# Where a unit's second scores and its scaling stand in the instruction order of an encoder step

## The chip, the core and the metric

One core of a Trainium2 chip runs the whole program. The metric is device time in microseconds of one execution. Engines: PE (TensorE, matmuls and transposes), DVE (VectorE), ACT (ScalarE), POOL (GpSimd) and SP, which only issues DMAs. All data are float32. Wide products use three passes on split numbers (high times high, high times low, low times high), which is why nearly every operand exists as a "hi" and a "lo" tile.

## The reference

One inference step of a four-layer encoder for 1024 prompt tokens and 32 decoded tokens (1056 together) with 512 cached positions. Every layer does the same around a different token mixer:

```
h = rmsnorm(x);  u = h @ w_in                 # mixer columns, memory queries, gate
br = mixer(...)                               # layers 0 and 3: A, layer 1: B, layer 2: C
mo = softmax(mq mem_k^T) mem_v                # M: 4 heads, 256 memory tokens
x  = x + (concat(br, mo) * silu(gate)) @ w_out
```

- A: 12 heads of 64, chunk-causal over a band of nine chunks of 64, with a relative bias.
- B: 6 differential heads: softmax(q0 k0) - lam * softmax(q1 k1) times a value of width 128, then an RMS norm.
- C: 12 latent heads; queries and keys have 64 plain and 32 rotary columns.

## The kernel before

Python builds one list, `plan.order`, and each engine's program walks through that list and issues only its own instructions. So the list fixes the order on every engine at once, and semaphores join the engines. Nothing is scheduled at run time.

**Jobs and units.** Per layer, attention is eight jobs: two M jobs (two memory heads each), then six of the mixer (two heads each, or one differential head). A job has five units (`units_of`, L169): four groups g of 256 queries and one of the 32 decoded tokens (g = 4). The units run as 0, 1, 2, 3, 4 in M and as 0, 2, 1, 3, 4 in the mixers. Units are written here by kind and group, as A2 for group 2 of an A job. A group has two tiles of 128 queries, and `width` is the number of keys that a tile sees: in M 256 and 256; in A 128 and 256 (A0), 384 and 512 (A1), 640 and 640 (A2, A3); in B and C 128 and 256 (group 0), 384 and 512 (group 1), 640 and 768 (group 2), 896 and 1024 (group 3). The decoded unit has one tile, of 544 keys or, in M, of 256.

**Steps of a unit.** Items of the list, with the lines where each engine does its part:
- `S` (scores): PE multiplies queries with keys into two score banks per lane (L1383); DVE adds the bias and takes a row minimum of the negated scores (L1154); ACT takes the exponential with its sum (L956). A tile of up to 512 keys takes one bank, tile 0 bank 0 and tile 1 bank 1; a wider one takes both, and so must wait until the tile before it has been biased.
- `N` (the scaling): DVE only. It waits for the exponentials, takes reciprocals (L1166) and multiplies the probabilities (L1177 and L1178; in B L1170, L1172 and L1174).
- `turn` (one chunk): PE transposes up to four 128x128 blocks of probabilities into a PSUM bank (L1395); ACT copies them out as hi (L965), and DVE subtracts for lo (L1184). The first turn of a unit waits for the `N` of its last tile.
- `pv`: PE multiplies values with the turned chunk into acc bank 0 (L1425). `evac`: DVE multiplies the result into the gate (L1208; in B L1203).
- `vt` (the values' transposition): PE L1407, ACT L974, DVE L1192.
- `part`: side products. While a job runs, the operands of the next one (q, k, v; in C uqe, uqo, ck, cv) are computed on PE in acc bank 1 (L1362), each a sum of 3 times 8 matmuls in A and B, which can be cut into 2 or 3 parts over the chunks. ACT reads each out (L875).
- `wsplit`: ACT makes w_hi (L915), POOL w_lo (L1228). `conv`: DVE casts the next job's queries and keys (L1136), POOL subtracts (L1246). `rot`: three DVE instructions that rotate C's queries (L1021, L1022, L1024). `vconv`: the cached values' split. `bsum` and `bmul`: B's norm (PE L1435, ACT L986 and L989, DVE L1215).

**The pipeline.** `unit` (L356) interleaves. While the chunks of unit u are turned and multiplied, the next unit nxt is scored and scaled. At chunk 0 stand the last `pv` of the unit before, its `evac`, the scores of nxt's tile 0, the values' transposition, the first part, and only then the scores of nxt's tile 1. Later chunks do `turn`, `pv` of the chunk before, and parts. The number n of chunks is 2 in M and 1 in the decoded units; A0 has 2, A2 and A3 have 5, A1 has 4; B0 has 1, B1 2, B2 3, B3 4; C0 has 2, C1 4, C2 6, C3 8. In units with n = 1 the `N` items stand behind all parts; with n = 2 they stand at the very end, behind the last part, the second `vt` and, in group 3, the first `conv`; with more chunks they stand in front of `turn`'s `pv` (tile 0, chunk 1) and behind it (tile 1, chunk 2).

Of the kernel before, what the change touches and what calls it, by code (L numbers as in the profile page):

```python
# [194 lines left out]
class Plan:  # L195
# [160 lines left out]
    def unit(self, u, prev, nxt, sides, jobs):  # L356

        order = self.order
        job, n = u.job, len(u.chunks)
        at = job.units.index(u)  # L360
        following = next((j for j in jobs if j.n == job.n + 1), None)
        parts = [[] for _ in range(n)]
        for i, s in enumerate(sides):
            own = list(range(n))[n * i // len(sides):n * (i + 1) // len(sides)] or [n * i // len(sides)]
            for p, c in enumerate(own):
                parts[c].append((s, p, len(own)))
        two = nxt is not None and len(nxt.tiles) == 2
        turns = [] if job is jobs[0] else list(range(len(V_TURNS[job.kind])))
        after_b = prev is not None and prev.job.kind == "B"
        if at == 4 and following is not None:  # L370
            order.append(("bprep", following))
        for c in range(n):
            self.turn(u, c)
            if c == 0:
                if prev is not None:
                    self.times_v(prev, len(prev.chunks) - 1)
                    order.append(("evac", prev))
                if nxt is not None:
                    self.scores(nxt, 0)
                if at == 0 and turns:  # L380
                    self.v_turn(job, 0)
                if at == 0 and following is not None:
                    order.append(("kload", following))
                if at == 3 and following is not None:
                    order.append(("bload", following))
                if parts[0]:
                    self.part(*parts[0][0])
                if two:
                    self.scores(nxt, 1)
                for x in parts[0][1:]:  # L390
                    self.part(*x)
                if n == 1 and nxt is not None:
                    order += [("N", nxt, t) for t in range(len(nxt.tiles))]
                if at == 1 and job is not jobs[0] and job.kind in "AB":
                    order.append(("vconv", job))
            else:
                if c == 1 and n > 2 and nxt is not None:
                    order.append(("N", nxt, 0))
                self.times_v(u, c - 1)
                if c == 2 and two:  # L400
                    order.append(("N", nxt, 1))
                if at == 3 and following is not None and c in (1, 3 if n > 4 else 2):
                    order.append(("conv", following, 0 if c == 1 else 1))
                for x in parts[c]:
                    self.part(*x)
            if after_b and c == min(1, n - 1):
                self.sum_of_squares(prev)
            if after_b and c == min(3, n - 1) and n != 2:
                order.append(("bmul", prev))
            if at == 0 and len(turns) > 1 and c == min(1, n - 1):  # L410
                self.v_turn(job, 1)
            if at == 1 and c < len(turns) - 2:
                self.v_turn(job, c + 2)
            if at == 1 and c == n - 1 and following is not None:
                order.append(("vload", following))
        if n == 2 and nxt is not None:
            order += [("N", nxt, t) for t in range(len(nxt.tiles))]
        if n == 2 and after_b:
            order.append(("bmul", prev))
        if at == 3 and following is not None and n == 2:  # L420
            order.append(("conv", following, 1))

# [1140 lines left out]
```

## Time and profile before

| what | us |
|---|---|
| median of 3 runs | 3563.18 |
| lowest and highest | 3560.32, 3565.85 |
| the profiled execution | 3553.51 |
| its span | 3551.7 |
| PE busy in it | 2924.7 (82%) |
| DVE busy | 1576.1 (44%) |
| ACT busy | 1221.1 (34%) |
| POOL busy | 832.2 (23%) |

The mean granted clock of TensorE in that execution was 0.884 of full speed. Busy time is what an engine spent in its instructions. In the views that list instructions, a bracket at the end of a row says how long the engine had been idle before it and which instruction let it go on.

### The profile page before, as it was taken

The numbers are of one execution on the slowest core, as the hardware profiler recorded it, in microseconds if no ns is written. First come the engines' busy times: TensorE is split into PE (matmuls) and PEld (weight loads), VectorE is DVE, ScalarE is ACT, GpSimd is POOL, SyncE is SP. The second block draws the span as 40 slices with busy tenths as digits, with TensorE's granted clock in tenths as the row PEclk, the third lists the DMA queues.
The fourth block names the chain that finished last, engine by engine and source line by source line (L and its number), as shares of the span: only waits on it lengthen the run. The fifth ranks groups of instructions, "written<-read, shape, count | busy, mean of one in ns | idle before, by whom it ended". The sixth has DMA issues, their size and how long they took to land.

```text
span 3551.7 us, 46359 instructions
## 1 busy us (share of the span) xinstructions
PE 2924.7 (82%) x18786; PEld 2708.6 (76%) x18786; DVE 1576.1 (44%) x3502; ACT 1221.1 (34%) x2680; POOL 832.2 (23%) x434
## 2 busy tenths in 40 slices
PE   5888899979888888869887667777779979999877
PEld 4787888869887777759787566666668978888777
DVE  7114555552215666661223256566551035555552
ACT  3323333332223444442232233333332233333331
POOL 7412112112412121213311222222104312122102
PEclk8998989989998999979997788788789989999979
DMA  3211111103111111103110000000013111111111
GB/s 140 91 42 47 38 38 47 38 26 122 56 36 52 43 51 43 55 20 120 60 36 31 24 10 8 6 8 6 13 64 94 44 33 47 41 52 38 47 61 61
DMA packets 55892, 167.90 MB, mean 47 GB/s; under 512 B 6464, under 2 KB 14272, under 8 KB 55168
## 3 DMA queue, kind: packets, MB, share of 16 engines
q1 hardware_dynamic: 55680, 164.94, 13.8%
q8 instruction: 149, 2.44, 0.3%
q14 instruction: 63, 0.52, 0.0%
HBM read 131.13 MB, written 33.79 MB: 46 GB/s over the span
## 4 chain that ended last, share of the span: by engine, by line
PE 68%; DVE 17%; ACT 8%; POOL 3%; issue 3%; DMA 0%; SPq 0%; DVEq 0%; ACTq 0%
PE acc L1362 32%; PE scores L1383 9%; PE acc L1425 9%; PE acc L1341 8%; PE turned L1395 5%; ACT prob L956 3%; DVE prob L1154 3%; DVE prob L1177 2%; PE scores L1294 2%; POOL h_split L1236 2%; DVE pt_split L1184 2%; DVE raw L1042 2%; DVE prob L1178 1%; ACT pt_split L965 1%; DVE prob L1172 1%
## 5 line engine op out<-in xcount | busy, mean ns | idle before, releaser
L1362 PE MATMUL acc<-h_split,w_hi 128*128 128x352 f32 (+3 forms) x5116 | 1280.8, 334 | 70.2 <-POOL w_lo L1228 40.1
L1362 PEld LDWEIGHTS acc<-h_split,w_hi 128*128 128x128 f32 x5116 | 915.0, 198 | 91.4 <-POOL w_lo L1228 43.5
L1228 POOL TENSOR_TENSOR w_lo<-w_raw,w_hi 128x1024 fp32r<-128x1024 f32 (+2 forms) x172 | 389.9, 2270 | 2013.0 <-ACT w_hi L915 2012.9
L1362 PE MATMUL acc<-h_split,w_lo 128*128 128x352 f32 (+3 forms) x2558 | 840.9, 329 | 0.0
L956 ACT ACTIVATE prob<-prob,stat 128x256 f32<-128x256 f32 (+9 forms) x576 | 386.7, 672 | 608.4 <-DVE stat L1154 608.4
L1425 PE MATMUL acc<-pt_split,v_split 128*64 128x256 f32 (+4 forms) x3486 | 515.4, 290 | 70.7 <-DVE pt_split L1184 64.7
L1395 PE MATMUL turned<-ident,prob 128*128 128x128 f32 (+2 forms) x1866 | 311.0, 294 | 298.6 <-DVE prob L1178 218.1
L1184 DVE TENSOR_TENSOR pt_split<-turned,pt_split 128x512 fp32r<-128x512 f32 (+4 forms) x564 | 303.0, 552 | 488.1 <-ACT pt_split L965 487.0
L1154 DVE CUSTOM_DVE_ANT_0 prob<-scores,bias 128x256 f32<-128x256 f32 (+9 forms) x576 | 343.3, 634 | 388.8 <-PE scores L1383 385.2
L1362 PEld LDWEIGHTS acc<-h_split,w_lo 128*128 128x128 f32 x2558 | 503.9, 197 | 0.0
L1395 PEld LDWEIGHTS turned<-ident,prob 128*128 128x128 f32 (+2 forms) x1866 | 229.0, 152 | 351.6 <-DVE prob L1178 235.7
L1425 PEld LDWEIGHTS acc<-pt_split,v_split 128*64 128x64 f32 (+1 forms) x3486 | 417.2, 168 | 95.4 <-DVE pt_split L1184 84.7
L965 ACT ACTIVATE pt_split<-turned 128x512 fp32r<-128x512 f32 (+4 forms) x564 | 260.9, 481 | 469.7 <-PE turned L1395 468.1
L1383 PE MATMUL scores<-k_split,q_split 64*128 64x512 f32 (+10 forms) x2196 | 355.0, 392 | 62.1 <-DVE stat L1154 31.6
L1383 PEld LDWEIGHTS scores<-k_split,q_split 64*128 64x128 f32 (+3 forms) x2196 | 232.3, 216 | 134.3 <-issue 61.1
L1341 PE MATMUL acc<-h_split,w_hi 128*128 128x352 f32 x1152 | 280.2, 327 | 9.2 <-POOL w_lo L1228 9.2
L915 ACT ACTIVATE w_hi<-w_raw 128x1024 fp32r<-128x1024 f32 (+2 forms) x172 | 166.5, 972 | 297.9 <-PE acc L1341 219.9
L1341 PEld LDWEIGHTS acc<-h_split,w_hi 128*128 128x128 f32 x1152 | 203.4, 192 | 10.2 <-issue 10.2
L1136 DVE CAST q_split<-q_raw 128x256 fp32r<-128x256 f32 (+1 forms) x52 | 28.1, 540 | 386.2 <-ACT q_raw L875 386.2
L1341 PE MATMUL acc<-h_split,w_lo 128*128 128x352 f32 x576 | 187.3, 325 | 0.0
L1294 PE MATMUL scores<-h_split,w_hi 128*128 128x352 f32 x512 | 133.8, 346 | 52.4 <-POOL h_split L1236 39.8
L1099 DVE TENSOR_TENSOR y_sb<-acc,y_sb 128x352 f32<-128x352 f32 x72 | 37.8, 525 | 253.5 <-PE acc L1341 253.5
(102 smaller groups left out, 2844.6 us busy)
## 6 DMA issues: line engine op xcount, KB each, us to landing
w_raw<-w SPq DMA_DIRECT2D x148, 512.0 KB, 3.5
x_scr<-y_sb SPq DMA_DIRECT2D x24, 528.0 KB, 5.3
y_sb<-x_scr SPq DMA_DIRECT2D x24, 528.0 KB, 5.4
bias<-rel_in SPq DMA_DIRECT2D x24, 320.0 KB, 4.2
raw<-kcache SPq DMA_DIRECT2D x18, 256.0 KB, 3.7
v_cache<-vcache SPq DMA_DIRECT2D x18, 256.0 KB, 3.7
y_sb<-x_in SPq DMA_DIRECT2D x8, 528.0 KB, 5.8
y_out<-raw SPq DMA_DIRECT2D x8, 528.0 KB, 2.7
```

Of the source, the lines that this page charges most:

```text
L915: act.activation(w_hi[:, n % 2, 0:wide], w_raw[:, n % 2, 0:wide], ACT.Copy).then_inc(whi_made.mark(n), 1)
L956: act.activation(p, p, ACT.Exp, scale=-1.0, bias=stat[0:tile.rows, i:i + 1], accum_out=stat[0:tile.rows, 8 + i:9 + i]).then_inc(exps_ready ...
L965: ins = act.activation(pt[0:rows, chunk.p % 2, 0, c0:c0 + n], t_ps[chunk.a % 2][0:rows, c0:c0 + n], ACT.Copy)
L1154: dve.tensor_tensor_reduce(out=prob[0:tile.rows, at:at + tile.width], in0=s_ps[lane][0:tile.rows, tile.at:tile.at + tile.width], in1=bias[ ...
L1184: ins = dve.tensor_tensor(pt[0:rows, chunk.p % 2, 1, c0:c0 + n], t_ps[chunk.a % 2][0:rows, c0:c0 + n], pt[0:rows, chunk.p % 2, 0, c0:c0 + ...
L1228: pool.tensor_tensor(w_lo[:, n % 2, 0:wide], w_raw[:, n % 2, 0:wide], w_hi[:, n % 2, 0:wide].bitcast(F32), ALU.subtract).then_inc(wlo_made ...
L1294: ins = pe.matmul(pair_banks[3 * i + c][:, 0:n], (w_hi, w_lo)[ws][:, w % 2, 128 * k:128 * k + 128], x[:, xs, k, a:a + n], start=k == 0 and ...
L1341: ins = pe.matmul(acc[i % 2][:, 0:n], (w_hi, w_lo)[ws][:, w % 2, 128 * k:128 * k + 128], h_v[:, xs, k, a:a + n], start=k == 0 and y == 0, ...
L1362: ins = pe.matmul(acc[s.bank][:, 0:s.cols], (w_hi, w_lo)[ws][:, w, 128 * k:128 * k + 128], x(xs, k), start=k == 0 and y == 0, stop=k == s. ...
L1383: ins = pe.matmul(s_ps[lane][0:tile.rows, tile.at + col:tile.at + col + n], q[rows, qs, tile.q0:tile.q0 + tile.rows], k[rows, ks, key:key ...
L1395: ins = pe.transpose(t_ps[chunk.a % 2][0:n, to:to + rows], prob[0:rows, at:at + n], ident[0:rows, 0:rows])
L1425: ins = pe.matmul(acc[0][0:width, dst:dst + w], v_sp[0:n, vs, block, 64 * lane:64 * lane + width], pt[0:n, chunk.p % 2, ps, src:src + w], ...
```

## The change

Only `unit` is changed. The scores of a next unit whose tiles are all at most 512 keys wide are issued for both tiles together, ahead of the values' transposition and of the first part. Where the next unit has one tile or is narrow, a unit with n = 1 issues `N` ahead of the parts; otherwise `N` follows the second scores directly. In units with n = 2 both `N` items move from the end to directly behind the second `turn`. With more chunks, the second `N` moves from behind `pv` to ahead of it. `bmul` of a unit with n = 2 moves into the loop. The order of the units, the table of side products per unit and all five engine programs are the same as before.

```diff
+        narrow = two and max(t.width for t in nxt.tiles) <= 512
         for c in range(n):
             self.turn(u, c)
             if c == 0:
...
                 if nxt is not None:
                     self.scores(nxt, 0)
+                if narrow:
+                    self.scores(nxt, 1)
...
+                if n == 1 and nxt is not None and not (two and not narrow):
+                    order += [("N", nxt, t) for t in range(len(nxt.tiles))]
                 if parts[0]:
                     self.part(*parts[0][0])
-                if two:
+                if two and not narrow:
                     self.scores(nxt, 1)
+                if n == 1 and two and not narrow:
+                    order += [("N", nxt, t) for t in range(2)]
                 for x in parts[0][1:]:
                     self.part(*x)
-                if n == 1 and nxt is not None:
-                    order += [("N", nxt, t) for t in range(len(nxt.tiles))]
...
             else:
-                if c == 1 and n > 2 and nxt is not None:
+                if c == 1 and nxt is not None:
                     order.append(("N", nxt, 0))
+                if c == (1 if n == 2 else 2) and two:
+                    order.append(("N", nxt, 1))
                 self.times_v(u, c - 1)
-                if c == 2 and two:
-                    order.append(("N", nxt, 1))
...
-            if after_b and c == min(3, n - 1) and n != 2:
+            if after_b and c == min(3, n - 1):
                 order.append(("bmul", prev))
...
-        if n == 2 and nxt is not None:
-            order += [("N", nxt, t) for t in range(len(nxt.tiles))]
-        if n == 2 and after_b:
-            order.append(("bmul", prev))
         if at == 3 and following is not None and n == 2:
             order.append(("conv", following, 1))
```

## Rows read from the trace of the kernel before

**Rows 1.** The page's busy times, then its chain that ended last, by engine.

```profile
PE 2924.7 (82%) x18786; PEld 2708.6 (76%) x18786; DVE 1576.1 (44%) x3502; ACT 1221.1 (34%) x2680; POOL 832.2 (23%) x434
...
PE 68%; DVE 17%; ACT 8%; POOL 3%; issue 3%; DMA 0%; SPq 0%; DVEq 0%; ACTq 0%
```

**Rows 2.** Waits of PE: us in total, times, longest us; last row 339:800 alone.

```profile
PE turned L1395 <- DVE prob L1178: 218.1, 64, 7.5
PE turned L1395 <- DVE prob L1174: 74.6, 24, 6.5
PE acc L1425 <- DVE pt_split L1184: 64.7, 45, 4.3
...
PE turned L1395 <- DVE prob L1178: 48.3, 12, 4.4
```

**Rows 3.** Timeline, one boundary into A0: start, us, instruction [idle before it].

```profile
491.14 0.55 PE L1383 MATMUL scores<-k_split,q_split 64*128 64x128 f32 x6
...
495.64 0.62 PE L1383 MATMUL scores<-k_split,q_split 64*128 64x256 f32 x6
...
497.20 2.46 DVE L1177 TENSOR_SCALAR prob<-prob,stat 128x128 f32<-128x128 f32 x1
497.23 2.34 POOL L1228 TENSOR_TENSOR w_lo<-w_raw,w_hi 128x1024 fp32r<-128x1024 f32 x1 [4.61 <-ACT w_hi L915]
...
500.63 1.12 PE L1395 MATMUL turned<-ident,prob 128*128 128x128 f32 x4 [4.37 <-DVE prob L1178]
501.40 3.58 PE L1425 MATMUL acc<-pt_split,v_split 128*64 128x32 f32 x30
...
504.91 2.18 PE L1383 MATMUL scores<-k_split,q_split 64*128 64x512 f32 x12
```

**Rows 4.** Timeline, the next boundary of such a job, from A0 into A2.

```profile
437.33 0.49 DVE L1184 TENSOR_TENSOR pt_split<-turned,pt_split 128x128 fp32r<-128x128 f32 x2 [1.39 <-ACT pt_split L965]
...
439.05 0.60 PE L1407 MATMUL turned<-ident,raw 128*128 128x128 f32 x4
...
440.32 0.69 DVE L1192 TENSOR_TENSOR v_split<-turned,v_split 128x512 fp32r<-128x512 f32 x1 [2.50 <-ACT v_split L974]
...
442.71 0.55 DVE L1178 TENSOR_SCALAR prob<-prob,stat 128x640 f32<-128x640 f32 x1
443.31 1.03 PE L1395 MATMUL turned<-ident,prob 128*128 128x128 f32 x4 [3.66 <-DVE prob L1178]
```

**Rows 5.** Timeline, B: the boundary into B0, then the one into B3.

```profile
1213.73 2.33 DVE L1172 TENSOR_SCALAR prob<-prob,stat 128x128 f32<-128x128 f32 x1
...
1217.61 0.69 PE L1395 MATMUL turned<-ident,prob 128*128 128x128 f32 x2 [4.32 <-DVE prob L1174]
...
1269.76 0.47 PE L1395 MATMUL turned<-ident,prob 128*128 128x128 f32 x1 [5.58 <-DVE prob L1174]
```

**Rows 6.** Timeline, C: the boundary into C0, then the one into C2.

```profile
2164.32 1.12 PE L1395 MATMUL turned<-ident,prob 128*128 128x128 f32 x4 [2.93 <-DVE prob L1178]
...
2184.54 1.25 DVE L1021 TENSOR_TENSOR raw<-q_even_raw,rope_sb 32x1056 f32<-32x1056 f32 x1 [1.44 <-ACT q_even_raw L875]
...
2187.52 1.25 DVE L1024 TENSOR_TENSOR q_even_raw<-q_even_raw,raw 32x1056 f32<-32x1056 f32 x1
...
2191.93 1.12 PE L1395 MATMUL turned<-ident,prob 128*128 128x128 f32 x4 [7.49 <-DVE prob L1178]
```

**Rows 7.** Timeline, M: around the decoded unit (M3 to M4), and into M2.

```profile
278.13 1.60 POOL L1246 TENSOR_TENSOR k_split<-raw,k_split 128x512 fp32r<-128x512 f32 x1
...
278.50 1.66 DVE L1136 CAST q_split<-q_raw 128x800 fp32r<-128x800 f32 x1
278.63 0.43 PE L1395 MATMUL turned<-ident,prob 32*128 32x32 f32 x4 [3.33 <-DVE prob L1178]
...
1058.01 0.66 PE L1395 MATMUL turned<-ident,prob 128*128 128x128 f32 x4 [1.11 <-DVE prob L1178]
```

**Rows 8.** Stretches: length, busy (x) of PE, PEld, DVE, ACT, POOL; PEclk, DMA, GB/s.

```profile
419.60:498.10 78.50, 71.04 (x517) 66.04 (x517) 40.18 (x104) 30.19 (x71) 14.43 (x9) 0.91 0.12 43
498.10:508.30 10.20, 7.67 (x52) 7.18 (x53) 4.56 (x11) 0.82 (x3) 1.48 (x1) 0.50 0.23 79
443.40:446.90 3.50, 3.50 (x18) 2.95 (x19) 1.84 (x4) 0.60 (x1) 0.00 (x0) 0.51 0.00 0
1214.90:1225.10 10.20, 7.49 (x36) 7.00 (x37) 4.96 (x13) 1.50 (x5) 1.08 (x1) 0.50 0.24 78
```

## The prediction

> **What bounds the kernel now.** The page first: PE is busy 82% of the span and carries 68% of the chain that ended last, DVE 17% [rows 1]. So PE sets the time, and what counts is where it stands still. The list of waits says on whom: 292.7 us (218.1 + 74.6) before a unit's first turn, on DVE's scaling, and 64.7 us before `pv`, on DVE's lo split [rows 2]. The timeline then places the first sum. I read it job by job, and every job of a kind repeats to 0.1 us, except the last of each layer, which has no side products. In the six A jobs of layer 0 there are 12 such waits of together 48.3 us (the last of [rows 2]), and layer 3 gives the same row: 4.37 us into each A0 [rows 3] and 3.66 into each A2 [rows 4]. B waits 4.32 into B0 and 5.58 into B3 [rows 5]; C 2.93 into C0 and 7.49 into C2 [rows 6]; M's first job of a layer 1.11 into each of three units [rows 7]. Elsewhere in an A job PE runs without a break: 71.04 us busy in a period of 78.5 [rows 8].
>
> The stretches show a second cost. Behind the wait at A0 the granted clock is 0.50 (the 1.2 GHz level) for 10.2 us, of which PE is busy 7.67; behind the one at A2 3.5 us at 0.51; behind the one at B0 10.2 us with 7.49 busy [rows 8]. The rest of the A job is at the upper level.
>
> **The change part by part.** No instruction is added or removed; each engine issues the same ones in another order. All counts are of this kernel's jobs.
>
> *Into A0 (12 times) and B0 (6).* Before: scores of tile 0 at 491.14, the v part between, scores of tile 1 at 495.64, so the part lasts 495.64 - 491.69 = 3.95 us. Then everything up to the first turn is exposed. It is long because the w_lo split on POOL (2.34 us) starts with DVE's scaling, and the 128-wide L1177 takes 2.46 us [rows 3], against 0.55 for a 640-wide L1178 [rows 4]. After: both scores stand together, the scaling is DVE's next work, and the part runs over it. The chain without the split is the old one, 500.63 - 496.26 = 4.37, less about 2.1 (2.46 less some 0.35, an estimate from the 0.55 of the wide one), so 2.3, and 0.6 more because tile 1 queues behind tile 0 on DVE and ACT: 2.9 us under a part of 3.95. No wait is left, and 1 us of slack. Gain 12 x 4.37 + 6 x 4.32 = 52.4 + 25.9 = 78. The split of w now falls behind the scaling, beside the lo split L1184.
> The GPSIMD Engine Reference of the Trainium skill (Key points) says that POOL's memory interface contends with Vector instructions in a two-port mode or with two SBUF inputs; L1177 beside L1228 agrees, and by that rule L1184, which reads PSUM, is not held.
>
> *A0 into A2 (10, and 2 without parts).* DVE ends the lo split of the second turn at 437.82, then idles until the values' transposition, issued by PE behind the part at 439.05, has come back as L1192 at 440.32; only then it scales, to 443.26 [rows 4]. After: scaling directly from 437.8. It takes 443.26 - 440.93 = 2.3 us (it overlaps L1192's end), so it ends at 440.15, and PE is ready at 439.65. The wait falls from 3.66 to 0.5: 10 x 3.1 = 31, and 0.7 each in the two jobs without a part, whose chain has only L1192 to lose: 1.4. L1192 moves behind the scaling, but its PSUM tile is only there at 440.3, so nothing waits for it: 32.
>
> *C0 into C2 (5 with the rotation; the layer's last job has none).* Before the scaling stand `rot` from 2184.54 to 2188.77 and L1192; the wait is 7.49 [rows 6]. The scaling fills the rest, 2191.93 - 2188.77 - 0.7 = 2.5 us. After: it starts when `rot` could, at 2184.5 less 1.44 idle = 2183.1 [rows 6], and ends at 2185.6; PE is ready at 2191.93 - 7.49 = 2184.44, so the wait falls to about 1. But `rot` (4.2), L1192 (0.7) and then the lo split of C2's first turn queue behind it on DVE, to 2191.2, and C2's second pair of transposes waits for that. PE has some 5 us of work until then (`pv`, two scores, a part), which before began only after the wait and now lies beside DVE's. So most of the 6.5 us are kept. The bounds are 1 (all of it late again at that turn) and 6.5; I take 5.5, nearer to the upper end, because the lo split that PE waits for would come at 2191.2, while before it could not start until ACT had read a transpose issued at 2191.93. 5 x 5.5, and 0.7 for the last job: 28.
>
> *C4 into C0 (5).* The cover is a cv part of 6 matmuls, 1.3 us, so 2.93 falls by 1 to 1.3: 5.
>
> *M (first job of each layer, three units).* The scores of tile 1 come 2.1 us earlier (half an mq part), but the turn in between pins the scaling behind its own lo split: of 1.11 [rows 7] 0.85 goes: 12 x 0.85 = 10. M3 to M4: the scaling passes the first `conv`. It gains 0.7 of 3.33, but the casts and POOL's two k and q splits start 0.9 later, the 800-wide cast that already stood 1.66 us beside POOL moves with them [rows 7], and the next job's first scores wait for POOL. Net loss 0.7 x 4 = 3, between 0 and 1.5 each.
>
> *No change:* into B3 (5.58) and B2: in both, between the old and the new place of `N` DVE has nothing, so its queue is the same. Tile 1's `N` ahead of `pv` is also nothing, since `pv` has no DVE part. `bmul` stays behind the same scaling. DMAs: SP's queue keeps its order, and w_raw's load follows the w_lo split as before.
>
> Stalls: 78 + 32 + 28 + 5 + 10 - 3 = 150. From this I take 5 for what shows up late next in C and around vconv, between 0 and 30: 145.
>
> **Rivals.**
> - *Stalls go, the clock stays.* For it: the 32-column matmuls. Against: in all 12 jobs the lower level begins inside the wait. 3563 - 145 = 3418. Chance 0.20.
> - *The whole lower level goes.* 3563 - 145 - 89 = 3329. Chance 0.14. "TensorE: Matmul & The Clock Gate" of the Trainium skill ("What's actually happening") says that the throttled state is the default and activity releases it, which would favour this one; that the lower level begins in the waits [rows 8] agrees.
> - *The moved scaling does nothing*, since ACT's exponentials and not L1192 or `rot` hold it. Against: L1192's idle bracket of 2.50 [rows 4]. Then 78 + 5 + 10 and half of the clock's 68 at A0 and B0: 3563 - 93 - 34 = 3436. Chance 0.07.
> - *What queues behind the scaling comes due elsewhere* (rot, L1192, conv): C and A2 give nothing, M loses, and the clock returns by half: 78 + 5 + 27 = 110 less 10, 3463. Chance 0.07.
> - *Slower: the scaling meets POOL.* Each meeting on the path costs 2.46 - 0.35 = 2.1 us [rows 3]. Today it meets 18 times. The order gains 200, so it turns slower from about 100 new meetings, of 172 splits of weights; at 110 it is 3563 - 200 + 231 = 3594. Against: most splits are issued behind a part's end, and the scaling now comes before. Chance 0.02.
> - *No effect beyond measurement:* chance 0.02.
>
> **How the numbers follow.** The forecast has 0.48 (its own range 3343 to 3393). Within 0.2% (7 us) is what a measurement of this kernel can't tell from no change. With the clock's two extremes, 3329 and 3418, 0.82 is covered; the range 3310 to 3432 holds them with their spread. Faster: all but 0.04; same 0.02, slower 0.02.
>
> **What would show it.** The waits of L1395 on L1178 and L1174 fall from 292.7 to about 110 (5.6 x 6 for B3, the M0 units at about 3, rests of 0.5 at A2, 1 to 1.9 in C). Right for A0: no bracket before its first turn, L1177 at 0.3 us, L1228 later than the scaling. Right for the clock: the stretch behind A0 at 0.9 or more, the mean over 0.91 against 0.884. Wrong: L1395 waiting at C2's second chunk for L1184 by 5 us or more, first scores of an M job waiting for POOL's k_split by over 2, or a clock that is still 0.50 behind A0.

## The result and the profile after

| | before | after |
|---|---|---|
| median, us (runs) | 3561.75 (4) | 3319.51 (4) |
| lowest, highest | 3554.15, 3565.85 | 3315.72, 3320.09 |
| the profiled execution | 3553.51 | 3319.59 |
| its span | 3551.7 | 3317.7 |
| PE busy in it | 2924.7 | 2822.7 |

The ratio is 0.932, with a 95% interval of 0.9302 to 0.9337. The lines of the kernel after stand one further down than before (L1395 is L1396, L1178 is L1179). From the page of the kernel after, its busy times:

```profile
PE 2822.7 (85%) x18786; PEld 2631.0 (79%) x18786; DVE 1540.5 (46%) x3502; ACT 1216.2 (37%) x2680; POOL 834.4 (25%) x434
```

Beside [rows 1] the counts are the same, so this is the same work. The span is 234.0 shorter: PE is busy 102.0 less, which must be the clock, as the instructions are the same, and idle 132.0 less (3551.7 - 2924.7 = 627.0 before, 495.0 after). The waits of PE in the kernel after (us in total, times, longest):

```profile
PE turned L1396 <- DVE prob L1179: 86.2, 55, 3.7
...
PE turned L1396 <- DVE prob L1175: 54.9, 24, 7.1
...
PE scores L1384 <- issue: 30.8, 8, 6.5
...
PE acc L1363 <- ACT w_rest L876: 13.4, 5, 2.7
```

The two waits on the scaling, 292.7 in [rows 2], are 141.1: 151.6 less. Two lines stand against that: `w_rest` is new (13.4), and "issue" was 24.6. These 13.4 + 6.2 = 19.6 are what is missing to 132.0: no other line of the list changes by more than 3.2, and together they change by 0.8.

One boundary into A0, to be read beside [rows 3] (start, us, instruction, idle before):

```profile
460.63 0.95 PE L1384 MATMUL scores<-k_split,q_split 64*128 64x128 f32 x12
...
463.17 0.29 DVE L1178 TENSOR_SCALAR prob<-prob,stat 128x128 f32<-128x128 f32 x1
...
464.42 0.35 DVE L1179 TENSOR_SCALAR prob<-prob,stat 128x256 f32<-128x256 f32 x1
...
465.48 0.60 PE L1396 MATMUL turned<-ident,prob 128*128 128x128 f32 x4
...
465.84 2.05 PE L1426 MATMUL acc<-pt_split,v_split 128*64 128x32 f32 x30
...
467.17 2.37 POOL L1229 TENSOR_TENSOR w_lo<-w_raw,w_hi 128x1024 fp32r<-128x1024 f32 x1 [5.07 <-ACT w_hi L916]
467.61 0.69 DVE L1185 TENSOR_TENSOR pt_split<-turned,pt_split 128x512 fp32r<-128x512 f32 x1 [2.84 <-ACT pt_split L966]
467.82 1.25 PE L1384 MATMUL scores<-k_split,q_split 64*128 64x512 f32 x12
```

Both tiles' scores stand in one row of 12. The scaling is over at 464.77, 0.7 before PE gets to the turn, which has no bracket. POOL's split starts 2.4 behind the scaling. The 30 short matmuls take 2.05 instead of 3.58.

Stretches of the kernel after (length, PE busy and its count, PEclk, DMA, GB/s): the 10.2 us behind that turn, then five periods of A in layer 0, of B, of C, and of A in layer 3, each from the first job's first turn of group 0 to the last job's:

```profile
465.48:475.68 10.20, 10.20 (x97) 1.00 0.30 106
...
334.97:662.79 327.82, 324.36 (x2567) 1.00 0.15 52
1053.00:1408.74 355.74, 315.52 (x2170) 0.95 0.15 53
1941.40:2397.26 455.86, 353.90 (x2157) 0.86 0.03 9
2809.64:3137.53 327.89, 324.43 (x2567) 1.00 0.15 52
```

The same periods in the kernel before:

```profile
343.05:739.80 396.75, 355.26 (x2567) 0.91 0.13 43
1140.58:1531.68 391.10, 332.82 (x2171) 0.91 0.14 48
2069.58:2556.57 486.99, 360.38 (x2158) 0.83 0.03 8
2973.30:3368.09 394.79, 353.29 (x2568) 0.92 0.13 43
```

Length less busy is idle, so each row parts its gain in two:

| five periods | shorter | idle less | busy less |
|---|---|---|---|
| A, layer 0 | 68.9 | 38.0 | 30.9 |
| B | 35.4 | 18.1 | 17.3 |
| C | 31.1 | 24.7 | 6.5 |
| A, layer 3 | 66.9 | 38.0 | 28.9 |

In A the clock is 1.00 over the whole stretch: nothing of the lower level is left. In C it only goes from 0.83 to 0.86.

### The profile page after: what moved, and what is told of

Its sections match the earlier page's. It is cut to its first block, busy times and chain, and to the rows that moved or that the text cites. A ratio compares the mean times of both kernels' runs of the same rounds, so it can differ in the third digit from the quotient of the medians.

```text
span 3317.7 us, 46359 instructions
## 1 busy us (share of the span) xinstructions
PE 2822.7 (85%) x18786; PEld 2631.0 (79%) x18786; DVE 1540.5 (46%) x3502; ACT 1216.2 (37%) x2680; POOL 834.4 (25%) x434
## 4 chain that ended last, share of the span: by engine, by line
PE 64%; DVE 17%; ACT 10%; issue 4%; POOL 4%; DMA 1%; SPq 0%; DVEq 0%; ACTq 0%
PE acc L1363 30%; PE acc L1342 9%; PE acc L1426 8%; PE scores L1384 8%; PE turned L1396 5%; ACT prob L957 5%; DVE prob L1155 3%; DVE pt_split L1185 3%; PE scores L1295 2%; POOL h_split L1237 2%; DVE raw L1043 2%; ACT pt_split L966 2%; DVE prob L1178 2%; DVE prob L1175 1%; POOL w_lo L1229 1%
## 5 line engine op out<-in xcount | busy, mean ns | idle before, releaser
L1363 PE MATMUL acc<-h_split,w_hi 128*128 128x352 f32 (+3 forms) x5116 | 1263.3, 330 | 84.4 <-POOL w_lo L1229 40.6
L1363 PEld LDWEIGHTS acc<-h_split,w_hi 128*128 128x128 f32 x5116 | 899.6, 194 | 109.0 <-POOL w_lo L1229 44.4
L1426 PE MATMUL acc<-pt_split,v_split 128*64 128x256 f32 (+4 forms) x3486 | 487.4, 280 | 73.5 <-DVE pt_split L1185 63.5
L1363 PEld LDWEIGHTS acc<-h_split,w_lo 128*128 128x128 f32 x2558 | 496.2, 194 | 0.0
L1426 PEld LDWEIGHTS acc<-pt_split,v_split 128*64 128x64 f32 (+1 forms) x3486 | 389.2, 156 | 98.5 <-DVE pt_split L1185 81.0
L1396 PE MATMUL turned<-ident,prob 128*128 128x128 f32 (+2 forms) x1866 | 301.4, 287 | 147.4 <-DVE prob L1179 86.2
L1396 PEld LDWEIGHTS turned<-ident,prob 128*128 128x128 f32 (+2 forms) x1866 | 227.2, 149 | 197.4 <-DVE prob L1179 103.8
L1384 PE MATMUL scores<-k_split,q_split 64*128 64x512 f32 (+10 forms) x2196 | 316.9, 364 | 69.3 <-DVE stat L1155 32.5
L1384 PEld LDWEIGHTS scores<-k_split,q_split 64*128 64x128 f32 (+3 forms) x2196 | 212.4, 200 | 125.0 <-issue 55.5
L1342 PEld LDWEIGHTS acc<-h_split,w_hi 128*128 128x128 f32 x1152 | 203.2, 192 | 10.2 <-issue 10.2
```

Of the source, the lines that this page charges most:

```text
L1342: ins = pe.matmul(acc[i % 2][:, 0:n], (w_hi, w_lo)[ws][:, w % 2, 128 * k:128 * k + 128], h_v[:, xs, k, a:a + n], start=k == 0 and y == 0, ...
L1363: ins = pe.matmul(acc[s.bank][:, 0:s.cols], (w_hi, w_lo)[ws][:, w, 128 * k:128 * k + 128], x(xs, k), start=k == 0 and y == 0, stop=k == s. ...
L1384: ins = pe.matmul(s_ps[lane][0:tile.rows, tile.at + col:tile.at + col + n], q[rows, qs, tile.q0:tile.q0 + tile.rows], k[rows, ks, key:key ...
L1396: ins = pe.transpose(t_ps[chunk.a % 2][0:n, to:to + rows], prob[0:rows, at:at + n], ident[0:rows, 0:rows])
L1426: ins = pe.matmul(acc[0][0:width, dst:dst + w], v_sp[0:n, vs, block, 64 * lane:64 * lane + width], pt[0:n, chunk.p % 2, ps, src:src + w], ...
```

## The experiments

The first three start from the kernel before: the first two do one part of the change each, the third moves only the split of w. The others start from the kernel after. Each time stands beside runs of the kernel before on the same chip (medians 3556.75, 3556.18 and 3556.41 in the three groups), and its ratio is to those.

**One part alone: the narrow scores together.**

```diff
+        narrow = two and max(t.width for t in nxt.tiles) <= 512
...
                     self.scores(nxt, 0)
+                if narrow:
+                    self.scores(nxt, 1)
...
-                if two:
+                if two and not narrow:
                     self.scores(nxt, 1)
```

> The kernel before with one part of the change alone: a narrow next unit's two score tiles are issued together; every scaling keeps its old place. Theory W (each wait brings its own stretch at the lower clock level, and takes it along when it goes): the waits into A0 and B0 go (about 76 us), M and C0 give 15, and the two lower stretches behind A0 and B0 return 68, so about 3403, with the 3.66 us wait into A2 and its 3.4 us at the lower level still there. Rival J (the level only comes back when all waits of a job are gone, or the 30 matmuls of 32 columns hold it down by themselves): about 3471, and the clock behind A0 still 0.50.

Measured: 3387.41, ratio 0.9527 (0.9511 to 0.9544), 169 us less. The stretches behind the turn into A0 and behind the one into A2:

```profile
478.54:488.74 10.20, 10.20 (x96) 1.00 0.31 106
496.76:500.26 3.50, 3.50 (x20) 0.50 0.00 0
```

Its terms had added up to 159 (76, 15 and 68), so it gave 10 more; PE is busy 82.6 less (2842.1), where 68 stood for the clock. The wait into A0 is gone and its lower stretch with it; A2's wait of [rows 4] is still 3.66 and keeps its own, which here lasts from 495.88 to 502.71. So each lower stretch belongs to its wait. The 30 short matmuls stand in the first of these rows at 1.00: their size does not hold the clock down.

**The other part alone: the scaling moved.**

```diff
-                for x in parts[0][1:]:
-                    self.part(*x)
                 if n == 1 and nxt is not None:
                     order += [("N", nxt, t) for t in range(len(nxt.tiles))]
+                for x in parts[0][1:]:
+                    self.part(*x)
...
-                if c == 1 and n > 2 and nxt is not None:
+                if c == 1 and nxt is not None:
                     order.append(("N", nxt, 0))
-                self.times_v(u, c - 1)
-                if c == 2 and two:
+                if c == (1 if n == 2 else 2) and two:
                     order.append(("N", nxt, 1))
+                self.times_v(u, c - 1)
...
-            if after_b and c == min(3, n - 1) and n != 2:
+            if after_b and c == min(3, n - 1):
...
-        if n == 2 and nxt is not None:
-            order += [("N", nxt, t) for t in range(len(nxt.tiles))]
-        if n == 2 and after_b:
-            order.append(("bmul", prev))
```

> The kernel before with the other part alone: the scaling moved as in the change, the second scores at their old place. Theory W: the wait into A2 falls from 3.66 to 0.4 (39 us) and its lower stretch goes (21), C2 gives about 32, the M4 units cost 3, so about 3473; A0 keeps its 4.37 us and its 10 us at 0.50. Rival J: no clock returns, about 3494. The savings of this one and of the scores alone should add to about 242, the whole change.

Measured: 3484.49, ratio 0.9798 (0.9781 to 0.9816), 72 less, where its terms (39, 21 and 32, less 3) had added up to 89. The clock gave what was expected: PE is busy 21.5 less (2903.2). The idle time did not: it is 47.1 less, where 68 stood. A2's wait is 0.46 and C2's 1.08, and the waits before first turns fall by 63.5 in all (to 154.4 + 74.8), but 16.4 of these come back elsewhere, 6.4 of them before the uqo part (`w_rest`) and 6.4 before the next M job's scores. Into A0 it shows what [rows 3] showed:

```profile
488.87 2.47 DVE L1173 TENSOR_SCALAR prob<-prob,stat 128x128 f32<-128x128 f32 x1
488.90 2.35 POOL L1224 TENSOR_TENSOR w_lo<-w_raw,w_hi 128x1024 fp32r<-128x1024 f32 x1 [4.61 <-ACT w_hi L911]
...
492.31 1.12 PE L1391 MATMUL turned<-ident,prob 128*128 128x128 f32 x4 [4.37 <-DVE prob L1174]
```

Beside their own runs of the kernel before the parts take 4.73% and 2.02%, together 6.75%, and the whole change takes 6.8%: the parts add up.

**Only the split of w behind the scaling.** In the decoded units and in B0 (n = 1), the scores stay apart.

```diff
+                    later = [x for x in order[mark:] if x[0] in ("wsplit", "wload")]
+                    order[mark:] = [x for x in order[mark:] if x[0] not in ("wsplit", "wload")] + later
```

> The kernel before with the weight split and the next weight load moved behind the scaling in the units of one chunk (A4, B4, C4), nothing else. It takes DVE's scaling away from POOL's split and ACT's w_hi from in front of the exponentials. If the 2.1 us beside POOL is a real price: waits into A0 and B0 fall from 4.4 to about 2.1, 41 us. If a wait of 2.1 us still brings the lower level: about 3521. If it doesn't: about 3453. If the overlap with POOL costs nothing on the path (the exponentials end last): 3555 or more.

Measured: 3519.76, ratio 0.9906 (0.9883 to 0.9928), 37 less, as the reading said by which a wait of 2.1 still brings the lower level (3521). The boundary into A0, and the stretch behind it:

```profile
493.56 0.29 DVE L1180 TENSOR_SCALAR prob<-prob,stat 128x128 f32<-128x128 f32 x1
...
495.14 1.12 PE L1398 MATMUL turned<-ident,prob 128*128 128x128 f32 x4 [2.51 <-DVE prob L1181]
...
495.90 3.58 PE L1428 MATMUL acc<-pt_split,v_split 128*64 128x32 f32 x30
```
```profile
495.03:501.80 6.77, 6.66 (x48) 0.50 0.33 116
```

The scaling beside POOL cost 4.37 - 2.51 = 1.86, and the prediction took 2.1. The edit also takes ACT's w_hi (1.05) from in front of tile 1's exponentials, but that is not what the wait was: in the kernel before these end at 498.13, and DVE, held beside POOL, is free for them only at 499.77. The clock is still at 1.2 GHz behind the shorter wait, and the short matmuls still take 3.58; that their size is not the reason, the first run shows and not this one.

**Is C2's new wait the scores' doing?** The kernel after has 2.7 for `w_rest` in C2. Its scores of C1 apart again:

```diff
-        narrow = two and max(t.width for t in nxt.tiles) <= 512
+        narrow = two and max(t.width for t in nxt.tiles) <= 512 and not (job.kind == "C" and at == 1)
```

> The kernel after, but in C2 units the two score tiles of C1 stand apart again, as before. Theory A (the new 2.7 us wait of the uqo part is ACT's queue: the exponentials of both score tiles stand ahead of the read that frees the bank, and wait for DVE's rotation): 5 x 2.7 = 13 less, 3306. Rival D (DVE's queue behind the rotation holds PE in any order): within 3 us of the kernel after, 3319.

Measured: 3322.08, ratio 0.9341 (0.9324 to 0.9357), no difference from the kernel after. It is not the place of C1's scores. The wait only splits up:

```profile
2054.92 0.51 PE L1363 MATMUL acc<-h_split,w_hi 128*128 128x264 f32 x2 [1.28 <-ACT w_rest L876]
...
2056.80 0.66 PE L1408 MATMUL turned<-ident,raw 128*128 128x128 f32 x4 [1.12 <-DVE v_split L1193]
```

**Is it the rotation, then?** Head 0's rotation (three operations of DVE) taken out of DVE's queue there and put behind the turn of C2's chunk 3; `streaming` is true inside `unit` only:

```diff
+            if s.what == "uqe" and self.streaming:
+                self.rot_later = ("rot", s.job, 0)
+            elif s.what in ("uqe", "uqo"):
...
             self.turn(u, c)
+            if c == 3 and self.rot_later:
+                order.append(self.rot_later)
+                self.rot_later = None
```

> The changed kernel, with one thing moved: the rotation of head 0 of the next C job, which DVE computes during C0's second chunk's turn and after (some 4.2 us of DVE, in four operations), is put behind the turn of C2's chunk 3, a unit in which DVE has room. Theory (DVE's queue holds PE at C0 to C2): in the changed kernel TensorE waits there 1.6 us at C2's second turn and 2.7 us for the uqo part, both behind that rotation; with it gone 2 to 4 us go in each of 5 jobs, so 10 to 20 us, 3300 to 3310. Rival (the rotation only moves the wait: the lo splits of C2 and the parts' evacuations queue behind it in its new place): within 3 us of the changed kernel, 3317 to 3323, with waits for L1185 in C2 longer than 1 us.

Measured: 3307.09 (3304.75 to 3307.59), ratio 0.9296 (0.9281 to 0.9311), 12.4 less than the kernel after. First the kernel after, then this one, from the rotation's last operation (in this one, from the lo split) to the uqo part:

```profile
2051.06 1.25 DVE L1025 TENSOR_TENSOR q_even_raw<-q_even_raw,raw 32x1056 f32<-32x1056 f32 x1
...
2055.02 0.61 ACT L957 ACTIVATE prob<-prob,stat 128x384 f32<-128x384 f32 x1 [5.19 <-DVE stat L1155]
...
2057.64 0.37 ACT L876 ACTIVATE w_rest<-acc 128x264 f32<-128x264 f32 x1
...
2058.06 0.39 PE L1363 MATMUL acc<-h_split,w_hi 128*128 128x264 f32 x1 [2.69 <-ACT w_rest L876]
```
```profile
2048.85 0.69 DVE L1193 TENSOR_TENSOR pt_split<-turned,pt_split 128x512 fp32r<-128x512 f32 x1 [0.78 <-ACT pt_split L974]
...
2053.55 0.37 ACT L884 ACTIVATE w_rest<-acc 128x264 f32<-128x264 f32 x1
...
2053.97 0.51 PE L1371 MATMUL acc<-h_split,w_hi 128*128 128x264 f32 x2 [0.60 <-ACT w_rest L884]
```

DVE's lo split now stands right behind its turn. The readout comes 4.1 earlier, 1.0 of it because C2's turn itself does (2047.52 against 2048.54). So the chain is: rotation, then DVE's bias for C1's tiles, then ACT's exponentials (idle 5.19 for them), and only behind these ACT's readout of the part, which frees the acc bank. The rotation starts it.

**The third M unit in the old order.**

```diff
+                held = n == 2 and at == 3
-                if c == 1 and nxt is not None:
+                if c == 1 and nxt is not None and not held:
...
+        if n == 2 and at == 3:
+            order.append(("N", nxt, 0))
```

> The changed kernel, with the scaling and transposition of the values of M4 put back behind the first convolution in the third M unit alone (M1, M2 keep the new order). Theory (the change loses a little there: M4's unit gets 0.8 us less wait at its own turn but the next job's first scores then wait 1.6 us for GpSimd's k_split): the wait at S(M0,0) goes from 1.58 to 0 and M4's goes from 2.50 back to 3.33; that is 0.75 us x 4 to 8 units, 3 to 6 us less than the changed kernel: 3314 to 3317. Rival (the two waits are one, whichever place it stands at): no difference, 3319 +- 2.

Measured: 3318.62 (3316.66 to 3322.26), ratio 0.9333 (0.9317 to 0.9348): no difference. First the kernel after, then this one:

```profile
273.18 0.43 PE L1396 MATMUL turned<-ident,prob 32*128 32x32 f32 x4 [2.50 <-DVE prob L1179]
...
274.70 1.26 POOL L1247 TENSOR_TENSOR k_split<-raw,k_split 128x512 fp32r<-128x512 f32 x1
...
276.06 1.65 PE L1384 MATMUL scores<-k_split,q_split 64*128 64x256 f32 x12 [1.58 <-issue]
```
```profile
273.44 1.60 POOL L1250 TENSOR_TENSOR k_split<-raw,k_split 128x512 fp32r<-128x512 f32 x1
...
273.94 0.63 PE L1399 MATMUL turned<-ident,prob 32*128 32x32 f32 x4 [3.32 <-DVE prob L1182]
...
275.98 1.65 PE L1387 MATMUL scores<-k_split,q_split 64*128 64x256 f32 x12
```

The next job's scores start at 276.06 or 275.98. What M4's turn gains, 0.82, its scores wait for again, since POOL's k_split ends 0.9 later (275.96 against 275.04). The wait of 1.58 put down to "issue" ends 0.1 behind that k_split.

**B3's wait, by POOL.** 5.58 into B3 is untouched by the change. The split in the two-chunk B unit moved behind the next unit's first turn:

```diff
             self.turn(u, c)
+            order += self.split_later
+            self.split_later = []
...
+                if job.kind == "B" and n == 2:
+                    self.split_later = [x for x in order[mark:] if x[0] in ("wsplit", "wload")]
+                    order[mark:] = [x for x in order[mark:] if x[0] not in ("wsplit", "wload")]
```

> The changed kernel, with GpSimd's split of the k part (its subtraction and the load behind it) moved in the wide B unit of two chunks from that unit's end to behind the first turn of the next one. Theory (the 5.58 us into B3 are DVE's 1024-wide scaling held beside GpSimd's subtraction, 2.50 us for 0.8): the wait falls by about 1.65 us to some 4.0, x5 jobs 8 us, 3311; if the lower clock behind that wait shortens too, up to 3305. Rival (the wait is set by the exponentials and sums, not by GpSimd): wait stays 5.5, time 3318 to 3322.

Measured: 3320.97, ratio 0.9336 (0.9321 to 0.9351). Here the mechanism held and the time did not move. The scaling before it in the kernel after, then in this one with the turn:

```profile
1238.49 2.50 DVE L1173 TENSOR_SCALAR prob<-prob,stat 128x1024 f32<-128x1024 f32 x1
...
1242.38 1.11 PE L1396 MATMUL turned<-ident,prob 128*128 128x128 f32 x4 [5.58 <-DVE prob L1175]
```
```profile
1240.73 0.74 DVE L1180 TENSOR_SCALAR prob<-prob,stat 128x1024 f32<-128x1024 f32 x1
...
1242.85 0.90 PE L1403 MATMUL turned<-ident,prob 128*128 128x128 f32 x3 [3.79 <-DVE prob L1182]
```

The wait is 1.79 shorter. Stretches of this kernel: the first 6 us of a B job in two, and the five B periods:

```profile
1194.39:1197.09 2.70, 2.57 (x22) 1.00 0.49 200
1197.09:1200.50 3.41, 3.41 (x21) 0.52 0.50 158
...
1054.23:1409.17 354.94, 323.56 (x2170) 0.93 0.15 53
```

Against the kernel after, PE is idle 8.8 less in the five periods (31.4 against 40.2) and busy 8.0 more (323.56 against 315.52), at a clock of 0.93 instead of 0.95. The busy time comes from two places, here in the third job of either kernel, this one and then the kernel after:

```profile
1241.60:1248.42 6.82, 5.57 (x28) 0.50 0.00 2
```
```profile
1240.27:1247.10 6.83, 4.72 (x25) 0.50 0.23 77
1267.60:1271.00 3.40, 3.40 (x19) 0.50 0.48 148
```

First, the lower stretch at the turn into B3 is as long as before. Most of the wait that went lay in it, so PE now does in it, at half the speed, what it did behind it at full speed: in the five periods that is 7.5 us more of busy time at 0.50, of which half, 3.7, is lost. Second, four times in the five periods a stretch of 3.4 stands behind the turn into the next B0, at a place where PE had not stood still for more than 0.34 us in the five before; in the kernel after it stands there once, in the third job. Three more of these cost 5.1, and 3.7 + 5.1 = 8.8 is near the 8.0 measured. Why the clock falls there, no run tells; it stays open.

**B3's wait, by the scores.** The change's own first part, used for B3's wide tiles too:

```diff
-        narrow = two and max(t.width for t in nxt.tiles) <= 512
+        narrow = two and (max(t.width for t in nxt.tiles) <= 512 or (job.kind == "B" and n == 2 and bool(sides)))
```

> The changed kernel, with the change's own first part used where it is not used yet: the two wide tiles of B3 are scored together, ahead of the k part, in the wide B unit of two chunks. The wait into B3 is 5.58 us in the changed kernel. Theory (what holds there is that the second tile's exponentials start late): the wait into B3 falls by about 4 us to 1.5; against it PE waits some 2 us for DVE's bias between the two scores, so 2 us x 5 jobs = 10 us less, and as much as 3.5 x 5 / 2 = 9 us less by the clock: 3300 to 3310. Rival (a wide tile's bias and exponentials need as long as what they are put ahead of, and the scores' wait takes all that is gained): 3317 to 3325.

Measured: 3307.50 (3306.27 to 3308.50), ratio 0.9298 (0.9284 to 0.9313), 12 less. Its second scores, the turn into B3, and the five B periods:

```profile
1225.67 1.88 PE L1384 MATMUL scores<-k_split,q_split 64*128 64x512 f32 x12 [2.31 <-DVE stat L1155]
...
1238.97 0.66 PE L1396 MATMUL turned<-ident,prob 128*128 128x128 f32 x4 [0.77 <-DVE prob L1175]
```
```profile
1053.21:1397.71 344.50, 313.91 (x2170) 0.97 0.16 55
```

4.8 less at the turn, 2.3 more at the scores: 9.6 of the 11.2 us in the five periods are idle time, 1.6 are clock.

**Both together**, the rotation later and B3's scores together:

> The changed kernel with both edits that gained by themselves: the rotation of head 0 of the next C job behind the turn of C2's chunk 3 (12.5 us less by itself), and B3's two wide tiles scored together ahead of the k part (12 us less by itself). They stand in different jobs. Theory (independent places, each gives what it gave alone): 3319.5 - 12.4 - 12.0 = 3295, range 3292 to 3299. Rival (the clock gives back a part, as it did where B3's wait fell by 1.77 us and the time not at all): 3300 to 3306.

Measured: 3296.18 (3292.42 to 3299.65), ratio 0.9272 (0.926 to 0.9285). That is 0.7% below the kernel after, with intervals apart, and the sum of the two singles to 1 us. With the third M unit in the old order as well:

> The same two edits, and the third M unit with its scaling back behind the first convolution (by itself 0.9 us less, inside the runs' spread). Theory (M4's wait back to 3.33, the next job's first scores from 1.58 to 0: 0.75 us less in each M pair, here or none): 0 to 3 us less than with two edits, 3292 to 3295. Rival (the clock takes it): the same as with two.

Measured: 3294.13 (3284.79 to 3299.84), ratio 0.9261 (0.9243 to 0.928): the same as with two.

## Why the prediction was right, and where it was off

The direction, the places and the order of the terms held; the time, 3319.5, lies near the lower end of 3310 to 3432, and below the forecast's own range of 3343 to 3393, which had 0.48. That the wide range held it is owed to the clock's extreme, 3329, which it was made to cover. The forecast of 3363 is 43.5 too high: 47 too little for the clock (55 against 102.0 of busy time), 13 too much for the stalls (145 against 132.0), and 9.5 between medians and the profiled executions. The step to name is the clock term.

- *Into A0 and B0, 78.* Right. A0's 4.37 is gone in all 12 jobs (0.2 is left in a layer's first). B has rests: B0 still waits 0.3 (1.4 in the first B job), and B1 1.2 where it had 0.5. The five B periods have 18.1 less idle time where 5 x 4.32 = 21.6 were forecast.
- *The split beside the 128-wide scaling.* Right and isolated: 1.86 measured for 2.1. By form, the 18 instructions of 128 columns at L1177, now L1178, took 1737 ns on average and now take 447.

- *A0 into A2, 32.* Right: 3.66 to 0.42. With A0 it makes 5 x (4.37 + 3.1) = 37.4 in five periods, and 38.0 were measured in either layer.
- *C0 into C2, 28, and C4 into C0, 5.* Into C0, 2.93 fell to 2.04, 4 in all. C2's wait itself fell about as forecast, from 7.49 to 1.1 or 1.6, and its second turn waits only 0.3. But the forecast looked for what is late next on DVE (the lo split), and it was one engine on: ACT's readout, 2.7 per job, 13.4 in all. Five periods had 24.7 less idle time where 5 x 6.5 = 32.5 stood in the sum. The bounds 1 and 6.5 held it.
- *M, 10, and M3 to M4, -3.* The waits of 1.1 into M1, M2 and M3 are 0.2, 0.6 and 0.6 in the first M job of each layer, 7 in all where 10 stood. M3 to M4 is no loss that can be seen, nor a gain (0.82 gained, 0.9 lost).
- *Late next, 5, between 0 and 30.* 19.6 (the 6.2 of it under "issue" are the next M job's scores, 4 x 1.58): the terms added up to 150, and the waits before first turns fell by 151.6, so the allowance was too small. The two numbers are not quite the same thing, since C2's term already held 1 us a job for lateness and M's the 3 for M4. The text's own sign "from 292.7 to about 110" did not follow from its sum, which gives 143; 141.1 came.
- *The clock, 55.* This is the term that was off: "Weight loads and short matmuls do not halve fully, so I take 55". Rows of short matmuls behind A0 do keep 54 to 57%: 2.05 instead of 3.58, 1.25 instead of 2.18 and 0.60 instead of 1.12. But over whole periods of A the work did halve. Inside the lower stretches of the kernel before, PE is busy 61.96 in the five A periods of layer 0 and 57.66 in those of layer 3; half of that is 31.0 and 28.8, and 30.9 and 28.9 came. In B and C it is rougher (half of the fall in such time is 13.7 and 9.8, and 17.3 and 6.5 came). In the whole execution PE's busy time at the lower level falls from 614.05 to 422.03; half of the difference is 96.0, and 102.0 came. So there was no reason to give up a third of the bound of 89. The bound itself was also too small, in two ways. It took one job's stretches for all, 5 x (7.67 + 3.5)/2 = 27.9 for five A periods, while in other jobs PE was busy 6.3 to 9.4 in the one behind A0 (in B 18.7 stood for 17.3). And C (6.5) and M had no term: 102.0 less the 83.5 of the four stretches (30.9, 17.3, 6.5, 28.9) leaves 18.5 for M and the jobs at a layer's ends, where 14.5 of the bound lay. The rival "the whole lower level goes" (0.14) is the case that came true in A, and its 3329 was the nearest number. By the rule of the Trainium skill that stood with it ("TensorE: Matmul & The Clock Gate", "What's actually happening"), that the throttled state is the default and activity releases it, A's 1.00 over 327.82 us agrees. The stretch at 0.52 behind 2.57 busy of 2.70, in the run on B3's split, is not accounted for by it.
- *Two readings.* "In all 12 jobs the lower level begins inside the wait" holds for 8. In the last A job of layer 0 and in the second, fifth and last of layer 3 the clock falls some 0.6 behind it (in the second the wait ends at 3050.59, and the upper level at 3051.24). And a layer's first job of B and C does not repeat the others: 4.95 into B0, 2.73 into C0 and 7.33 into C2.
- *The rivals.* "The clock stays" falls with the 1.00 behind A0; "the moved scaling does nothing" with its 72 us alone; the slower one because POOL's split comes behind the scaling in the timeline. "What queues behind comes due elsewhere" came true for 19.6 us and not as the rival had it: A2's wait fell to 0.42, and C gave 24.7. "No effect" falls with the ratio. The sign for the mean clock, "over 0.91", was not quite met: it was 0.910 against 0.884.

## What to carry to other kernels

Price a wait on the bounding engine with the slow stretch behind it: here 132 us of waits brought 102 us more, taking the wait out entirely gave the clock back, and making it 2.51 instead of 4.37 did not. When an instruction is moved ahead in a queue, follow what it passes over two engines, not one, and then ask for each remaining wait whether the same resource ends the next one too: if it does (M4), moving it gains nothing. A shorter wait is not yet a shorter time: confirm it with length and busy of the whole period, as B3's split shows, where the time won lay inside a stretch at the lower level that did not get shorter.

## What was not expected of the hardware

- A wait of 2.51 us into A0 is followed by 0.50 over all of the 6.77 us looked at, one of 2.05 into C0 in the kernel after by 10.24 at 0.50 (2120.91 to 2131.15), and one of 2.31 us before B3's second scores, with one of 1.18 ahead of it, by this stretch:

```profile
1226.76:1230.17 3.41, 3.41 (x15) 0.53 0.00 0
```

  Waits of 0.4, 0.6 and 1.2 (A2, M2, B1) are passed at 1.00.
- The clock also fell to 0.52 where PE had been busy 2.57 of 2.70 us. With the lower stretch at B3 that kept its length, this took back 8.0 of 8.8 us in B.
- A DVE multiplication with one tensor in SBUF took 2.47 us for 128 columns beside POOL's 2.35 and 2.50 for 1024 columns beside its 2.56: it is held until POOL is done, at either width. It is not always DVE that waits: at 1957.70 in the kernel after, DVE's scaling of 768 columns began 0.03 ahead of POOL and took 0.61, and POOL's split of 256 columns took 1.16; in the next job the split took 0.72 and the scaling 1.15. The lo split, which reads PSUM, took 0.69 beside POOL's 2.37.
